# Weighting the attention rows of the second pair of heads on ScalarE

## What is computed

```
def masked_softmax(s, mask):
    m = jnp.max(s, axis=-1, keepdims=True)
    e = jnp.where(mask, jnp.exp(s - m), 0.0)
    return e / jnp.maximum(jnp.sum(e, axis=-1, keepdims=True), 1e-30)

def nsa_merge(g, o_cmp, o_slc, o_win, dtype):       # each o_* is softmax(...) @ values of its branch
    o = g[0] * o_cmp + g[1] * o_slc + g[2] * o_win
```

## Time and profile before

| | us |
|---|---|
| time, median of 3 runs | 2047.46 (2047.34 to 2050.22) |
| the profiled execution | 2048.04 |
| its span | 2046.3 |
| busy in the span: TensorE / VectorE / ScalarE / GpSimd | 1914.0 / 729.9 / 488.8 / 565.1 |
| `phase_attend`, first matmul to the start of the next stage | 402.0 to 698.3 |
| busy in it: TensorE / VectorE / ScalarE / GpSimd | 250.3 / 207.1 / 163.0 / 179.6 |

### The profile page before, as it was taken

How to read it: one execution, slowest core, us unless ns; L and a number is a source line. 1 busy time by engine, 2 the same in 40 slices (tenths; PEclk the granted TensorE clock), 3 DMA queues, 4 the chain that set the end, 5 groups by cost and what they waited for, 6 DMA issues and landing times. The chain is left out here.

```text
span 2046.3 us, 26094 instructions
## 1 busy us (share of the span) xinstructions
PE 1914.0 (94%) x10662; PEld 1552.6 (76%) x10662; DVE 729.9 (36%) x1621; ACT 488.8 (24%) x1093; POOL 565.1 (28%) x468
## 2 busy tenths in 40 slices
PE   7999999879998599999979959999999999999996
PEld 5888887745555377777758858888888888888885
DVE  4321213578776334234222074310331233213323
ACT  3311212356555334343320050000100010000002
POOL 2212222157665321111103143221111112222214
PEclk9999998889999799999989989999999999999998
DMA  4011121120000475656504010111111111111112
GB/s 132 28 56 52 58 51 57 58 91 1 1 1 1 153 242 197 221 176 230 182 13 142 21 42 21 42 42 42 46 58 42 42 41 42 42 42 42 42 53 83
DMA packets 113631, 149.74 MB, mean 73 GB/s; under 512 B 21584, under 2 KB 99320, under 8 KB 105256
## 3 DMA queue, kind: packets, MB, share of 16 engines
q1 hardware_dynamic: 104296, 80.95, 13.2%
q0 software_dynamic: 9216, 67.11, 9.7%
HBM read 139.96 MB, written 12.27 MB: 74 GB/s over the span
## 5 line engine op out<-in xcount | busy, mean ns | idle before, releaser
L278 PE MATMUL PS<-Z,ring 128*128 128x258 f32 x1152 | 258.2, 380 | 0.0
L1809 PE MATMUL PS<-Z 128*128 128x256 f32 (+1 forms) x1024 | 244.6, 385 | 0.0
L278 PEld LDWEIGHTS PS<-Z,ring 128*128 128x128 f32 x1152 | 218.1, 189 | 33.0
L278 PE MATMUL PS<-hT,ring 128*128 128x258 f32 x992 | 226.1, 385 | 7.7 <-DMA ring<-in_w_out 7.2
L1809 PEld LDWEIGHTS PS<-Z 128*128 128x128 f32 x1024 | 186.4, 190 | 42.8 <-issue 20.3
L278 PEld LDWEIGHTS PS<-hT,ring 128*128 128x128 f32 x992 | 189.9, 192 | 37.5 <-DMA ring<-in_w_out 7.2
L241 POOL TENSOR_TENSOR Z<-ring 128x512 f32<-128x512 f32 x36 | 47.0, 1305 | 601.6 <-PE PS L278 532.5
L2355 ACT ACTIVATE Z<-PS 128x516 f32<-128x516 f32 x80 | 48.0, 600 | 647.0 <-PE PS L278 647.0
L278 PE MATMUL PS<-Z 128*128 128x258 f32 x832 | 187.1, 380 | 0.0
L2375 DVE TENSOR_TENSOR Z<-PS,Z 128x516 f32<-128x516 f32 x96 | 66.8, 696 | 314.9 <-PE PS L278 314.9
L278 PEld LDWEIGHTS PS<-Z 128*128 128x128 f32 x832 | 157.5, 189 | 23.9
(11 more groups left out here) (379 smaller groups left out, 2790.4 us busy)
## 6 DMA issues: line engine op xcount, KB each, us to landing
ring<-in_w_ff_up SPq DMA_DIRECT2D x32, 512.0 KB, 5.3
ring<-in_w_ff_down SPq DMA_DIRECT2D x32, 512.0 KB, 4.0
ring<-in_w_in SPq DMA_DIRECT2D x9, 1024.0 KB, 5.1
X<-in_x_prompt SPq DMA_DIRECT2D x8, 1024.0 KB, 11.2
srow<-in_state_nsa_win SPq DMA_DIRECT2D x16, 256.0 KB, 5.3
out_y_prompt<-X SPq DMA_DIRECT2D x8, 512.0 KB
out_win_sample<-in_state_nsa_win SPq DMA_DIRECT2D x1, 4088.0 KB
out_kv_prompt<-Z SPq DMA_DIRECT2D x8, 256.0 KB, 2.0
```

The lines of the kernel that those rows point to most:

```text
L278: last = nc.tensor.matmul(M.PS[:, bank_of(M, n, e) + c, 0:CW], a[:, k, :], b[:, k, c * CW:(c + 1) * CW], start=e in (M1, M2, M5) and k == ...
L1809: last = nc.tensor.matmul(out, w1s[:, v, half, 2 * r + e, :], x2[seg][:, r, v, :, e, half:half + SEG[seg]], start=(j == 0), stop=(j == 15))
```

## The change

The pieces that VectorE weighted go to ScalarE, as a copy with a scale column. The rule by which the six pieces of an m are divided changes as well: in the units of query tiles 0, 1 and 2 (n = 0, 1, 12 to 15) ScalarE takes all three pieces of kvh 1, where before VectorE took three in unit 0 alone and GpSimd had the selected one in the others. So 66 instructions leave VectorE and 10 leave GpSimd, and ScalarE gets 76. On ScalarE the weighting of (n + 1, 0) stands in the middle stage of iteration n, after the stage's copy and before its exponentials, and that of (n + 1, 1) at the end of the iteration. The first transpose of a unit waits for `norma` in place of `normv`.

```diff
-    def weighted(n, on_vector):
+    def weighted(n, on_scalar):
         return [(kvh, br, c, w) for kvh in range(KVH) for br, c, w in pieces(n)
-                if (kvh == 1 and (n == 0 or br != SEL)) == on_vector]
+                if (kvh == 1 and (br != SEL or SU[n][0] <= 2)) == on_scalar]
...
-    normv = M.sem("probs_weighted_dve")
+    norma = M.sem("probs_weighted_act")
...
-                for kvh, br, c, w in weighted(n, on_vector=False):
+                for kvh, br, c, w in weighted(n, on_scalar=False):
...
+            def weigh(n, g):
+                m = 2 * n + g
+                act.wait_ge(rcr, m + 1)
+                for kvh, br, c, w in weighted(n, on_scalar=True):
+                    last = nc.scalar.activation(p_of(n, g, kvh)[:, c:c + w], p_of(n, g, kvh)[:, c:c + w], ACT.Copy,
+                                                scale=rc[:, m % NSLOT, br, kvh:kvh + 1])
+                last.then_inc(norma, 1)
+
             for n in range(-2, NSU):
...
                     if n >= 1 and i == 0:
                         y_out(n - 1)
+                    if i == J // 2 and 0 <= n + 1 < NSU:
+                        weigh(n + 1, 0)
                     for k in share(12, i, J):
...
                             exps(n + 2, 0, k - 6)
+                if 0 <= n + 1 < NSU:
+                    weigh(n + 1, 1)
             y_out(NSU - 1)
...
                 nc.vector.tensor_tensor(r, r, gates, ALU.mult).then_inc(rcr, 1)
-                dve.wait_ge(rcr, m + 1)
-                for kvh, br, c, w in weighted(n, on_vector=True):
-                    last = nc.vector.tensor_scalar(p_of(n, g, kvh)[:, c:c + w], p_of(n, g, kvh)[:, c:c + w],
-                                                   rc[:, m % NSLOT, br, kvh:kvh + 1], None, ALU.mult)
-                last.then_inc(normv, 1)
...
                     pe.wait_ge(normd, 2 * n + 2)
-                    pe.wait_ge(normv, 2 * n + 2)
+                    pe.wait_ge(norma, 2 * n + 2)
```

## The result

The changed kernel takes 2028.09 us, the median of four runs (2025.40 to 2031.08), against 2047.59 for the kernel before beside it: a ratio of 0.9901, 95% interval 0.9888 to 0.9915, or 20 us less. The direction was right and the size too small. 2035.2 was forecast, 12 us less.

The account below looks back on a forecast made before the run. The attention stage was taken as a loop of TensorE waits, the last-ending one counting. Gains of 8.7 + 1.4 + 2.15 + 0 = 12.3 us gave 2035.7, or 2035.2 against the median; range 2028 to 2045.

Parts of the forecast that it names:

- (d): 76 weightings arriving on ScalarE: absorbed by its idle time, price 0, bounds -0.6 to +0.5 us.
- opening: TensorE's wait for VectorE's copy opening iterations 3 and 7 to 12, behind a weighting pair; 7.1 us gained in all.
- hold-up: GpSimd's first piece slowed by VectorE's weightings beside it; 0.36 us for each long unit.
- middle: Odd-half weightings before mid-iteration copies; waits counted only in iterations 6 to 9 and 11, 1.6 us together.
- division: GpSimd giving up second-pair selected pieces in units 1 and 12 to 15: 1.3 at T(13), 0.15 at T(14), 0.7 at the end.
- (a): 66 weightings leaving VectorE, where they stood before copies TensorE waits for; 7.1 plus 1.6, together 8.7 us.
- the clock: Half-clock stretches behind TensorE's waits, each costing half its length, 1.7 us; change in them taken as 0.
- (b): GpSimd's first piece no longer held up, counted at T(4), T(5), T(6), T(11): 4 x 0.36 = 1.4 us.
- (c): GpSimd giving up the second pair's selected piece in units 1 and 12 to 15, 10 instructions; 2.15 us.
- the rival with 0.10: Three or four of the stage's half-clock stretches vanish: 5 us more, 2030; chance 0.10.
- Rival 1: Only GpSimd counts: other waits end as late behind VectorE's copies, leaving 3.6 us, 2043.9; chance 0.12.
- Rival 2: ScalarE takes the place: at 2.5 us a pair, +8.5 us, 2056; sign turns from about 1.9; chance 0.11.

Follow-up runs that it names:

- after_again: The changed kernel run once more without an edit; 2026.17 us, ratio 0.9892.
- behind_copy: The kernel before, all weightings still on VectorE and the division unchanged, but placed behind the copy they stood in front of; 2033.7 us, ratio 0.9933.
- even_half: The kernel before with only the weightings of g = 0 moved to ScalarE, g = 1 left on VectorE, division as before; 2036.72 us, ratio 0.9947.
- old_division: The changed kernel with the selected pieces divided between GpSimd and ScalarE as before; 2030.92 us, ratio 0.9920.
- left_out: The changed kernel with ScalarE's 76 weightings left out altogether; 2028.08 us, ratio 0.9891.
- the filled kernels: The kernel before and the changed kernel, each with idle TensorE transposes ahead of waits at T(n); 2037.70 us (0.9948) and 2020.47 us (0.9871).
- before_again: The kernel before run again without an edit; 2047.44 us, ratio 0.9998.
- act_longer: The changed kernel with ScalarE's weightings cut into instructions of 64 columns, a pair taking 2.7 us; 2051.28 us, ratio 1.0016.

## Why the prediction was right in kind and short in size

The iterations from T(n) to T(n+1) show the prediction's sum term by term, if they are freed of half-clock stretches: each duration is from an execution that has none in that iteration. Only iteration 0 is never free of them; there the shortest of each kernel stands.

| iteration | before | after | gain | forecast | its terms |
|---|---|---|---|---|---|
| 0 to 2 | 43.16 | 43.34 | -0.2 | 0 | (d) |
| 3 | 19.11 | 16.88 | 2.2 | 1.64 | opening 1.28, hold-up 0.36 |
| 4, 5 | 43.48 | 42.34 | 1.1 | 0.72 | hold-up 2 x 0.36 |
| 6 | 22.02 | 21.32 | 0.7 | 0.34 | middle |
| 7, 8 | 43.96 | 40.88 | 3.1 | 2.30 | openings 0.92, middles 0.23 |
| 9 | 22.04 | 19.98 | 2.1 | 1.79 | 1.18, 0.61 |
| 10 | 18.82 | 17.17 | 1.7 | 1.53 | 1.17, hold-up 0.36 |
| 11 | 16.31 | 15.75 | 0.6 | 1.04 | 0.84, 0.20 |
| 12 | 13.55 | 11.08 | 2.5 | 2.12 | 0.82, division 1.3 |
| 13 | 10.10 | 9.75 | 0.4 | 0.15 | division |
| 14 and end | 6.81 | 6.12 | 0.7 | 0.7 | division |
| sum | 259.4 | 244.6 | 14.7 | 12.3 | |

With T(0), 0.4 us earlier, the moved work is worth 15.1 us. The half-clock stretches behind T(0) cost 9.5 us in the profiled execution of before, 7.3 in that of after and 4.5 in after_again; the stage is 17.4 and 19.8 us shorter. So the forecast's 12.3 us missed on two terms: the moved work is 15.1, mostly since (a) is 10.8 and not 8.7, and the clock is 2 to 5 us and not 0. In detail:

- *What bounds the stage.* Right. The waits in front of VectorE's copies made the loss; behind_copy takes most of it away without another engine.
- *(a), 8.7 us.* The right mechanism, a term too small, and the first that failed. Iterations 3 and 6 to 12 gained 12.7 us; without 1.2 for the division and 0.36 twice for the hold-up that is 10.8. even_half has the openings at 7.8, not 7.1; between it and after, the middle waits of iterations 6 to 9 hold 2.1 where 1.4 was summed; and iterations 3 and 12 gained some 0.7 from the odd half, where nothing was counted. What was wrong is the size of a wait, taken from TensorE's matmul row. In iteration 7 of before that row says 0.92 us for the opening and 0.23 for the middle; TensorE's weight-load row for the same transposes says 1.16 and 0.46:

```profile
555.28 0.44 PE L1661 MATMUL PS<-ident,Z 128*128 128x128 f32 x2 [0.92 <-DVE X L1613]
...
555.28 0.20 PEld L1661 LDWEIGHTS PS<-ident,Z 128*128 128x128 f32 x2 [1.16 <-DVE X L1613]
...
567.43 0.31 PEld L1661 LDWEIGHTS PS<-ident,Z 128*128 128x128 f32 x3 [0.46 <-DVE X L1613]
```

  The experiments bear the weight-load row out. even_half, which takes away the opening wait alone, has iteration 7 at 21.77 us, 1.13 less than before, and after, which takes away both, at 21.32, another 0.45 less. The ends of matmuls are modelled, and in these two places they cover 0.24 and 0.23 us of the wait.
- *(b), 0.36 us each.* The piece lost exactly that (3202 to 2847 ns). Iterations 4 and 5 gained 0.46 and 0.68, so the step is right and a little small. That the pair on VectorE is dear because of its second piece is not borne out: in behind_copy the piece of 63 takes 0.24 us, the first one takes longer, and the pair still takes 1.20. The Trainium skill (SBUF — State Buffer, "SBUF: two separate sides") says that the lock between the two engines is held for a whole instruction. The 2847 agree with a hold-up by VectorE that is gone. For VectorE it does not hold here: its pieces end at 521.32 and 513.24, with the piece of GpSimd beside them running until 523.00 and 514.63.
- *(c), 2.15 us.* Right, 2.0 by the iterations, old_division against after.
- *(d), 0 us.* Right within its bounds of -0.6 to +0.5: T(0) gained 0.4, iterations 0 to 2 lost 0.2, and in the other iterations ScalarE's work cost nothing. The 1.5 us of left_out are counted from after; at T(0), T(1), T(3) and T(14) ScalarE's end stands where GpSimd's stood in before. T(3) was taken back as told, T(0), T(1), T(3) and T(14) wait for ScalarE as told. Its cover in the middle stage shrank by just the pair: the copy of iteration 7 that had 1.71 us of idle time before it has 0.75 in after, behind a weighting that holds ScalarE from 550.30 to the next start at 551.25, 0.95 us. TensorE waits for ScalarE's copies 0.5 us in all.

```profile
550.30 1.05 ACT L1551 ACTIVATE X<-X,misc 128x640 f32<-128x640 f32 x2
551.25 0.33 ACT L1527 ACTIVATE X<-X,misc 128x63 f32<-128x63 f32 x1
551.49 0.19 ACT L1527 ACTIVATION_READ_ACCUMULATOR X<-X,misc 128x1 f32 x1
552.43 0.60 ACT L1538 ACTIVATE X<-PS 128x512 f32<-128x512 f32 x1 [0.75 <-PE PS L1668]
```

- *The clock, taken as 0.* Wrong; this is the second term that failed, and the larger one. It was the rival with 0.10 that came true beside the forecast: 2.2 us in the profiled execution of after, 5.0 in after_again, about 4 by the filled kernels. That each 3.4 us cost 1.7 was nearly right, 1.36 to 1.64. Which waits are followed by half clock, the rows still don't tell. The wait of 1.44 us at T(4) has half clock behind it in before and none in before_again or in after (1.43 us); that of 2.23 us at T(6) has 6.8 us in after and 3.4 in after_again.
- *Rival 1* would have left 3.6 us: refuted by behind_copy and even_half. *Rival 2* is a real mechanism with the wrong premise. At a pair of 2.7 us, act_longer loses 23 us against after; the prediction's two points (12.3 us lost at 1.9, 20.7 at 2.5) run on to 23.5. That the two agree so well is in part luck, since some 5 of the 23 us are clock, which the line does not hold. The sign turns later than at 1.9 us, since there were 20 us to lose and not 12: by the same line at some 2.4 us, an estimate. ScalarE's pair is 0.95. The Trainium skill (Trainium Architecture — The Big Picture, "The five engines, in one table") keeps simple arithmetic away from ScalarE, per element. Instruction by instruction the rows agree in direction (818 against 554 ns); for this kernel it did not matter, as left_out shows.
- *The range.* Its lower end took in the clock's 5 us on top of 12.3, but not that the 12.3 could be short as well; both came, and the time fell about 1 us below it.

Open: why the times of after and old_division may differ by up to 3 us more than their iterations tell, which waits have half clock behind them, and what decides between 3.4 and 6.8 us of it.

## What to carry to other kernels

Ask of each instruction not what it costs but what stands behind it in its queue: 1.3 us of weighting in front of a copy that TensorE waits for cost 1.3 us. Behind the copy it cost 0.7 us in iteration 3, 0.2 in two more and nothing in the others, and on an engine that is slower at it but idle there some 1.5 us in the whole stage. When a helper's work is moved, read the receiver's idle time at the very places where the work will stand, and the last thing it does before the unit's turn. Sum waits from the weight-load row as well as from the matmul row, and leave room below for the clock, since shorter waits can give back half-clock time that no row promises.

## What the runs showed of the hardware

- A wait of TensorE costs more than its length when a stretch of half clock follows. In this stage one of 3.4 us costs 1.36 to 1.64 us, and up to 10 us in all hung on them. Idle transposes in the wait, 94 in before and 87 in after, took away all of those at the places filled, and one came anew where none was filled: the stage went from 295.8 to 289.0 and from 276.4 to 271.7 us. No rule for when a stretch comes is worked out here.
- A multiply on VectorE beside one on GpSimd was held up here, and by how much went with the size of GpSimd's piece. In behind_copy, where it starts 0.43 us behind GpSimd's, VectorE's piece of 640 takes 1035, 930, 824 and 716 ns beside GpSimd pieces of 1024, 896, 768 and 640, where the earlier trace rows have 554: 0.83 ns more for each element of GpSimd's piece (1035 - 716 over 384 elements), which itself takes 2.5 ns per element (2847 - 1885 over the same 384). In before, where VectorE starts 0.06 us ahead, its next piece (63 elements) is the one held, up to 1.11 us, and GpSimd's is held 0.36 us. ScalarE's pieces of 63 take 336 ns in the mean (the group shown above), as its exponentials of 63 do. The piece of 640 beside that of 640:

```profile
586.06 0.72 DVE L1607 TENSOR_SCALAR Z<-Z,misc 128x640 f32<-128x640 f32 x1
```

- ScalarE's instructions of 64 columns last 336 ns but start 0.25 us apart (100 of them, 24.8 us busy), so that their mean overstates what a row of them costs:

```profile
L1553 ACT ACTIVATE Z<-Z,misc 128x64 f32<-128x64 f32 x100 | 24.8, 336 | 0.0
```
